# Low parts of the lower halves of the second-weight pairs: negated high part by ScalarE, raw weights added by a transfer

## What is computed

```python
x = x + jnp.square(jax.nn.relu(h2 @ w_mlp_in[layer])) @ w_mlp_out[layer]      # first block
hdn = jnp.square(jax.nn.relu(jnp.einsum('bld,df->blf', u, w_ff1)))            # second block
h = h + jnp.einsum('blf,fd->bld', hdn, w_ff2)
```

## Time and profile before

| | us |
|---|---|
| median of 3 runs (1407.33 to 1407.54) | 1407.5 |
| span of the profiled execution | 1405.3 |
| TensorE busy | 1397.8 (99%) |
| VectorE busy | 921.2 (66%) |
| ScalarE busy | 596.3 (42%) |
| GpSimd busy | 211.8 (15%) |

### The profile page before, as it was taken

The page is one execution under the profiler, slowest core; times in us unless marked ns, Lnnn a source line. Parts: engine busy times, 40 slices in busy tenths (PEclk is TensorE's granted clock), DMA queues, the critical chain, the costliest instruction groups (busy, mean ns, idle before and its releaser), DMA issues.

```text
span 1405.3 us, 21789 instructions
## 1 busy us (share of the span) xinstructions
PE 1397.8 (99%) x8746; PEld 1184.5 (84%) x8746; DVE 921.2 (66%) x1248; ACT 596.3 (42%) x842; POOL 211.8 (15%) x215
## 2 busy tenths in 40 slices
PE   9999999999999999999999999999999999999998
PEld 7898779777888989989888997778888998989886
DVE  6635433765767858577656778556756967758775
ACT  4324531553445434353244435344434535344353
POOL 4000000000022302211433020000022221302310
PEclk9999999999999999999999999999999999999999
DMA  5223123211336845635233322232225773927573
GB/s 183 90 91 113 61 68 102 72 31 59 100 99 169 188 133 144 157 114 153 91 96 99 92 63 82 64 103 90 90 90 139 180 162 113 214 91 191 138 175 109
DMA packets 154860, 161.61 MB, mean 115 GB/s; under 512 B 4010, under 2 KB 144660, under 8 KB 154788
## 3 DMA queue, kind: packets, MB, share of 16 engines
q1 hardware_dynamic: 122868, 129.12, 28.9%
q0 software_dynamic: 31904, 31.46, 12.3%
q10 hardware_dynamic: 16, 0.00, 0.0%
HBM read 157.68 MB, written 2.10 MB: 114 GB/s over the span
## 4 chain that ended last, share of the span: by engine, by line
PE 99%; ACT 0%; DVE 0%; issue 0%; POOL 0%; POOLq 0%; ACTq 0%
PE ps L2355 63%; PE ps L2420 17%; PE ps L2351 4%; PE ps L2377 4%; PE ps L2493 3%; PE ps L2748 1%; PE ps L2563 1%; PE ps L2777 1%; PE ps L2763 1%; PE ps L2867 1%; PE ps L2652 0%; PE ps L2695 0%; PE ps L2674 0%; PE ps L2949 0%; PE ps L2540 0%; PE ps L2713 0%
## 5 line engine op out<-in xcount | busy, mean ns | idle before, releaser
L2355 PE MATMUL ps<-AA,wh 128*128 128x512 f32 x1440 | 453.5, 396 | 0.0
L2355 PE MATMUL ps<-BB,wh 128*128 128x512 f32 x1088 | 342.2, 396 | 0.2 <-issue 0.2
L2355 PEld LDWEIGHTS ps<-AA,wh 128*128 128x128 f32 x1440 | 267.4, 188 | 62.6 <-DVE wl L1449 0.8
L2355 PE MATMUL ps<-AA,wl 128*128 128x512 f32 x720 | 283.4, 394 | 0.0
L915 ACT ACTIVATE wh<-raw 128x1024 fp32r<-128x1024 f32 (+2 forms) x149 | 141.5, 950 | 259.8 <-PE ps L2355 206.0
L2355 PEld LDWEIGHTS ps<-BB,wh 128*128 128x128 f32 x1088 | 202.2, 188 | 49.3 <-issue 1.6
L2355 PE MATMUL ps<-BB,wl 128*128 128x512 f32 x544 | 213.9, 393 | 0.0
L1449 DVE TENSOR_TENSOR wl<-raw,wh 128x1024 fp32r<-128x1024 f32 (+2 forms) x149 | 169.9, 1140 | 60.6 <-ACT wh L915 60.3
L2355 PEld LDWEIGHTS ps<-AA,wl 128*128 128x128 f32 x720 | 135.4, 188 | 30.9
L2355 PEld LDWEIGHTS ps<-BB,wl 128*128 128x128 f32 x544 | 102.3, 188 | 23.3
L2420 PE MATMUL ps<-Hl,wh 128*128 128x256 f32 x384 | 107.8, 281 | 0.0
(11 more groups left out here) (408 smaller groups left out, 2410.6 us busy)
## 6 DMA issues: line engine op xcount, KB each, us to landing
raw<-in_w_in SPq DMA_DIRECT2D x38, 1024.0 KB, 5.4
raw<-in_w_ff SPq DMA_DIRECT2D x31, 1024.0 KB, 5.4
raw<-in_w_mlp_in SPq DMA_DIRECT2D x16, 1024.0 KB, 5.4
raw<-in_w_mlp_out SPq DMA_DIRECT2D x16, 1024.0 KB, 5.3
zf<-in_w_mlp_out POOLq DMA_DIRECT2D x48, 256.0 KB, 4.8
zf<-in_w_ff POOLq DMA_DIRECT2D x48, 256.0 KB, 4.6
raw<-in_w_out SPq DMA_DIRECT2D x8, 1024.0 KB, 5.4
arena<-in_x SPq DMA_DIRECT2D x4, 512.0 KB, 7.1
```

Of the source, the lines that this page charges most:

```text
L2355: last = pe.matmul(dense_psum(t_ps, kind), a[:, k, :], b[:, o0 + k, col0:col0 + S1], start=start, stop=stop)
```

## The change

The low part of A12 and A22 is no longer a subtraction by VectorE. ScalarE's `lower(q)` writes the high part into `wh` as before and then, in a second activation with scale -1, the negated high part into `wl`; it raises the new semaphore `neg_hi`. GpSimd waits for it (`lower_low`) and issues an adding transfer of the raw weights, from `raw` to `wl`, 128 partitions of 4 KB, 512 KB. When it has landed (`lower_lo`), `wl` holds the low part. TensorE waits for `lower_lo` ahead of A12. VectorE's `lower_landed(q)` waits for `lower_lo` too and then raises `lo_ready` by 2, for SyncE. Slot 1 keeps the layout of `raw`, which TensorE reads in blocks of 128 columns.

```diff
@@ GpSimd, strassen_sums
                     for q in range(4):
                         s13_sums(which, c, q)
+                        if 4 * c + q >= 2:
+                            lower_low(which, 4 * c + q - 2)
+                for u in (4 * (CHUNKS - 1) - 2, 4 * (CHUNKS - 1) - 1):
+                    lower_low(which, u)
...
+            def lower_low(which, u):
+                pool.wait_ge(neg_hi, so_far(which, 4) + u + 1)
+                pool.dma_start(wl[:, 1, :].bitcast(F32), lower_pair(MLPS[which][2] + 4 + u % 4), accum_op=ALU.add).then_inc(lower_lo, 16)
@@ ScalarE, strassen_chunk
                 def lower(q):
-                    act.activation(lower_slot(wh), lower_pair(p0 + 4 + q), ACT.Copy).then_inc(hi_ready, 2)
+                    act.activation(wh[:, 1, :], lower_pair(p0 + 4 + q), ACT.Copy).then_inc(hi_ready, 2)
+                    act.activation(wl[:, 1, :], lower_pair(p0 + 4 + q), ACT.Copy, scale=-1.0).then_inc(neg_hi, 1)
@@ VectorE, strassen_chunk
-                def lower(q):
-                    dve.wait_ge(hi_ready, t + 8 + 2 * q + 2)
-                    dve.tensor_tensor(lower_slot(wl), lower_pair(p0 + 4 + q), lower_slot(wh), ALU.subtract)\
-                       .then_inc(lo_ready, 2)
+                def lower_landed(q):
+                    dve.wait_ge(lower_lo, 16 * (so_far(which, 4) + q + 1) + 64 * c)
+                    dve.sem_inc(lo_ready, 2)
...
-                    if j == 7:
-                        lower(0)
...
                         first_sums(q + 1)
+                    lower_landed(q)
                     dve.wait_ge(blk_done, done + 6)
...
-                    else:
-                        lower(q + 1)
@@ TensorE, strassen_chunk
-                    pe.wait_ge(lo_ready, t + 8 + 2 * q + 2)
+                    pe.wait_ge(lower_lo, 16 * (so_far(which, 4) + q + 1) + 64 * c)
                     block_product(A12_, B21, g1, False).then_inc(blk_done, 1)
```

More of the change, by code:

```diff
@@ L369, in build @@
             sem("hid_sq"), sem("t_diff"), sem("t4_diff"), sem("hid_hi"), sem("hid_lo"))
+        neg_hi, lower_lo = sem("neg_hi"), sem("lower_lo")
         g_landed, ts_sum, ts3_sum = sem("g_landed"), sem("ts_sum"), sem("ts3_sum")
@@ L460, in lower_pair, with lower_block @@
         def lower_pair(p):
-            return raw[:, p % 2, :].rearrange("p (k n) -> p k n", k=KT)[:, 4:8, :].rearrange("p k (o n) -> p o k n", o=2)
-        def lower_slot(w):
-            return w[:, 1, :].rearrange("p (o k n) -> p o k n", o=2, k=4)
+            return raw[:, p % 2, DM:2 * DM]
+        def lower_block(w, o):
+            return w[:, 1, :].rearrange("p (k o n) -> p o k n", o=2, k=4)[:, o]
         def blk(ap):
@@ L2410, in strassen_chunk @@
                 upper, lower = slice(0, S1), slice(S1, DM)
-                A12_, A22_ = (blk(wh[:, 1, upper]), blk(wl[:, 1, upper])), (blk(wh[:, 1, lower]), blk(wl[:, 1, lower]))
+                A12_, A22_ = ((lower_block(wh, o), lower_block(wl, o)) for o in range(2))
                 S4_, S2_ = (blk(wh[:, 0, upper]), blk(wl[:, 0, upper])), (blk(wh[:, 0, lower]), blk(wl[:, 0, lower]))
```

## The result

| | median us | runs | ratio to before | 95% interval |
|---|---|---|---|---|
| before | 1407.52 (1407.33 to 1407.66) | 4 | | |
| changed | 1509.66 (1503.3 to 1517.1) | 4 | 1.0728 | 1.0695 to 1.0762 |

The change costs 102 us, 7.3%. The forecast was 1491 us, with a range from 1457 to 1532. The profiled execution of the changed kernel took 1503.3 us, its span 1501.6, which is 96.3 us more than the 1405.3 of before. It is the fastest of the four; what makes the median 6.4 us longer than it, no trace shows.

The account below looks back on a forecast made before the run. TensorE, 99% busy, bounds the kernel; stalls for the new transfer, 4 x 16 + 2 x 9.8 = 84 us, on the 1405.3 us span plus 2.2 between span and median give 1491 us, range 1457 to 1532.

Parts of the forecast that it names:

- What bounds the kernel: TensorE, busy for 99% of the span at full clock, longest wait 1.7 us, at the program's start.
- VectorE's part: The dropped subtraction, 1.22 us in 24 pairs, 29 us beside TensorE's work with no wait behind it: worth nothing.
- ScalarE's part: The second activation, 0.95 to 1.07 us, delays nothing TensorE waits for but stands in the chain to the new transfer.
- GpSimd's place as the step that costs: In GpSimd's queue, pair 2's new transfer has its operand at +12.3 but is issued behind S1/S3 transfers at +17.11.
- The cover of the loads: Loads released by VectorE's wait start 4 to 5 us later, take 5.3 us, are needed after 8.75: cost zero.
- The size of L: Time from the new transfer's issue to its landing, 8 us behind an adding pair, 5.7 with nothing ahead.
- The alternation: Neighbouring pairs' stalls sum to 8 us: 4.8, 3.2, 4.8, 3.2 in chunks that another of the same MLP follows.
- L - 4.8: Lower bound of a pair's stall after a late pair, because the operand then comes later than the queue.
- Size alone: Rival: a transfer costs a fixed start plus its bytes, adding or not; 51 us in all, 1458.5 us, chance 0.04.
- Quick addition: Rival: new transfer lands in 6.1 us behind a pair, 4.2 alone; 61 us in all, 1468.5 us, chance 0.20.
- Crowded queue: Rival: new transfer lands in 10.5 us behind a pair, 5.7 alone; 112 us in all, 1520 us, chance 0.13.
- The clock: Rival: TensorE's clock halves in new gaps; one slow product in 20 gaps costs 28 us, 1519 us, chance 0.13.

Follow-up runs that it names:

- the kernel with the old pair 0: Changed kernel with the new transfer issued between plain and adding pairs, and pair 0 of each chunk back on VectorE's subtraction: 1437.12 us, ratio 1.0208.
- the kernel with the filling and the transfer between the pairs: Changed kernel with the new transfer issued between plain and adding pairs, and 28 more matmuls before TensorE's wait in pair 0 of every chunk: 1464.74 us, ratio 1.0394.

## Why the prediction was right, and where its terms were off

**What bounds the kernel, VectorE's part, ScalarE's part.** Right. A kernel with no subtraction at all is no faster, and the second activation costs some 3 us.

**GpSimd's place as the step that costs.** Right in kind, and shown: the transfer moved ahead of the adding pair gives back 37 us. It is 37 of the 102, though, and not all that pairs 1 to 3 lose. The forecast had every transfer of pairs 1 to 3 held by the queue where S1 and S3 stand ahead of it, and named an issue at ScalarE's activation as the sign against. Of these 14 transfers six go at the activation and eight are held, for 16.5 us in all. Ten, the eight among them, go right behind an adding pair and pay for that in the landing too, 6.7 us or more against 4.6 in pair 0.

**The cover of the loads.** Half right. TensorE has no wait of more than 0.5 us for A11 or for a slab's weights, nor for the tail behind the last chunk, which is what the forecast had claimed. What it had not seen is that the load, started 4 to 5 us later, now runs beside the plain pair on whose landing GpSimd waits.

**The size of L.** The loop is the best place to check it. The forecast gave 19.96 + 8 = 27.96 us; the chain shows 30.67. Piece by piece:

| piece | forecast | measured | difference |
|---|---|---|---|
| A12 to the end of the next pair's fourth product | 8.75 | 11.42 | +2.7, the slow clock |
| VectorE to the end of L1560 | 3.82 | 3.84 | 0 |
| L1560 to the plain pair | 0.30 | 0.29 | 0 |
| plain pair to adding pair | 4.50 | 6.56 | +2.1, the load beside it |
| adding pair to the new issue | 2.62 | 1.55 | -1.1 |
| new issue to A12 | 8 | 7.01 | -1.0 |

The forecast's pieces are from the earlier trace rows. The issue term was a misreading: the 2.62 us of the row for an adding pair hold the trailing part of its second issue, and the next transfer can start after two slots of 0.78 us. The two mistakes on the transfer itself made the loop 2.1 us too long, and the two that were missed, clock and load, 4.8 us too short. In pair 0 the transfer took 4.6 us rather than 5.7, and TensorE waited 3.8 rather than 4.8.

**The alternation.** The forecast had stalls of 4.8, 3.2, 4.8, 3.2 in a chunk. Measured in the second chunk, with the fall of the clock behind each (2.5, 1.5 and 2.5 us), are 6.3, 3.3, 6.8 and nothing. After so late an A12 in pair 2 the operand of pair 3 comes later than the adding pair ahead of it, so the transfer goes alone. My floor, L - 4.8, used the L of the crowded queue where the one of the empty queue (4.8 us) holds; with that it is 0, as measured there. In the fifth chunk it is pair 2 that finds the queue empty and waits for 0.33 us, and pair 3 waits for 6.34.

**The rivals.** "Size alone" has fallen: 4.5 us is the fastest landing of 512 KB, against the 2.7 us that it gave for half a load, and a landing behind an adding pair is nearly 3 us longer even for 64 KB. The rule of the Trainium skill (DMA: Bandwidth & Descriptors, Anatomy of one DMA), from which I had estimated 3.2 us, does not describe an adding transfer of this size in this trace, which takes at least 4.5; the one of 64 KB landed in 2.3 to 2.6 when nothing was ahead of it. "Quick addition" came nearest on the transfer itself: 4.5 us alone against its 4.2, and behind an adding pair 7.0 - 1.1 = 5.9 us, counted from where the forecast took the issue to be, against its 6.1. Its 61 us of stalls are also nearest to the 64.5 us of waits. "Crowded queue" was true of the plain pair rather than of the new transfer. **The clock** was true too, and to treat it as a rival of the forecast rather than as a term in it was the main mistake: here it comes with 14 of the 19 waits. A fall costs an estimated 1.3 to 2.6 us where I had 1.43, at 14 places rather than 20. That the time lies in the range owes something to luck, since two errors partly cancelled: 64.5 us of waits, at 19 places, instead of 84 at 24, and 31.7 us of longer busy time, some 25 of them the clock, instead of none. They leave the forecast 12.2 us below the profiled execution; the other 6.4 of its 18.7 us are the distance of the median from that execution.

**What stays open.** Why the clock falls at once after some gaps, later after others, and at some not at all, these runs do not tell. The 29 us that the kernel with the old pair 0 leaves in pairs 1 to 3 are no wait in GpSimd's queue: it waits for ScalarE ahead of all 18 new transfers. They lie between the negated part and the landing, 4.5 to 7.6 us; how much of that is the addition and how much the traffic beside it, these runs do not divide.

## What to carry to other kernels

Before a transfer replaces an elementwise instruction, follow it to its place in the queue and to whoever needs it: an operation of 1.2 us beside other work was exchanged for one of 4.5 to 7 us on the path of the only engine that is full. A stall of a full TensorE has to be priced with the clock that it loses afterwards, here 1.3 to 2.6 us for each of 14 falls beside 19 waits. And where a stall feeds itself through a loop over every other pair, a gap closed in one loop opens in the other; look for the sum over both before expecting a gain.

## What the runs showed of the hardware

- An adding transfer from SBUF to SBUF of 512 KB (128 rows of 4 KB) landed in 4.5 to 5.2 us when the adding pair ahead of it had been issued more than 4 us before, and in 6.7 to 7.4 right behind an adding pair of 2 x 256 KB. Issued between the plain and the adding pair it took 4.5 to 8.3 us. With 64 KB it was 2.3 to 2.6 us alone and 4.8 to 5.3 right behind an adding pair.
- Two plain transfers of 256 KB from HBM, in the chunks of the changed kernel, had landed 3.0 to 3.3 us after their issue ended when the nearest load of 1 MB started 5 us ahead of them or 1.8 to 2.1 us behind, and 5.0 to 6.5 us when it started within 1.0 us of them.
- TensorE's granted clock fell from its 2.4 GHz to its 1.2 GHz level at 14 of 19 waits of the changed kernel. In the chunk above it was down for about 26 matmuls of 128x256 from the end of the waits of 3.81 and 4.31 us on, and for 16 matmuls from 1.5 us after the one of 1.83 us. It did not fall at waits of 2.92 and 3.22 us. In the kernel with the filling and the transfer between the pairs, a gap of 3.77 us was followed by 1.2 us at the full clock before it fell, and one of 3.27 us by no fall at all in the next 4.5 us:

```profile
483.50:488.00 4.50, 4.50 (x38) 4.50 (x39) 3.68 (x5) 2.34 (x3) 1.55 (x2) 1.00 0.80 247
507.80:509.00 1.20, 1.19 (x10) 1.19 (x11) 0.00 (x0) 0.00 (x0) 0.63 (x1) 1.00 0.94 113
509.00:511.60 2.60, 2.60 (x15) 2.60 (x14) 0.69 (x1) 0.00 (x0) 0.00 (x0) 0.51 1.06 175
```

These are windows of that kernel, from the end of the two gaps on; the third number from the right is the granted clock.
